# Weights of the last chunk's first block product through the staging buffer, and halves of products read ahead of activation low parts

## What is computed

```python
    merged = jax.nn.sigmoid(ga) * y_a + jax.nn.sigmoid(gb) * y_b
    x = x + merged @ w_o

    h2 = rmsnorm(x, g_ffn)
    x = x + jnp.square(jax.nn.relu(h2 @ w_up)) @ w_down
    return x
```

## Time and profile before

| | us |
|---|---|
| median of 3 runs | 1888.57 (1887.17 to 1890.57) |
| the profiled execution | 1888.48 |
| its span, first to last instruction | 1886.4 |
| TensorE busy | 1865.5 (99% of the span) |
| VectorE busy | 1255.6 (67%) |
| ScalarE busy | 837.2 (44%) |
| GpSimd busy | 129.4 (7%) |

### The profile page before, as it was taken

One profiled execution on the slowest core, in us unless ns is written; L12 is line 12 of the kernel. 1 busy time (PEld: TensorE's weight loads), 2 busy tenths in 40 slices (PEclk: granted clock), 3 DMA queues, 4 the chain that ended last, 5 costly groups with the idle time before them and its releaser, 6 DMA issues.

```text
span 1886.4 us, 22990 instructions
## 1 busy us (share of the span) xinstructions
PE 1865.5 (99%) x9064; PEld 1549.7 (82%) x9064; DVE 1255.6 (67%) x1858; ACT 837.2 (44%) x1234; POOL 129.4 (7%) x104
## 2 busy tenths in 40 slices
PE   9999999999999999999899999999999999999997
PEld 7888888887888888888788888888878888888886
DVE  5356778767456666767863568788665575676777
ACT  7325465464223333434472255554632233344344
POOL 0001111100000000000000112111000000000100
PEclk9999999999999999999999999999999999999999
DMA  4543233333333465564626333233243334655655
GB/s 146 200 159 120 83 89 118 90 93 104 120 101 114 132 134 136 150 136 125 145 88 240 96 104 104 77 118 104 68 146 101 101 112 113 141 148 134 134 147 121
DMA packets 208235, 230.64 MB, mean 122 GB/s; under 512 B 13440, under 2 KB 160640, under 8 KB 207360
## 3 DMA queue, kind: packets, MB, share of 16 engines
q1 hardware_dynamic: 190512, 194.74, 32.7%
q0 software_dynamic: 16896, 33.56, 10.5%
q10 hardware_dynamic: 720, 0.87, 0.1%
HBM read 215.38 MB, written 13.77 MB: 121 GB/s over the span
## 4 chain that ended last, share of the span: by engine, by line
PE 85%; issue 6%; DVE 4%; DMA 3%; ACT 2%; POOL 0%; SPq 0%; POOLq 0%; ACTq 0%; DVEq 0%
PE pj L1816 19%; PE pj L1818 19%; PE pj L1817 19%; DMA gh<-in_w_down 2%; PE yr L2122 1%; PE yr L2124 1%; PE yr L2126 1%; DVE w_lo L1140 1%; PE pt L2122 1%; PE pt L2124 1%; PE pt L2126 1%; PE sc L2122 1%; PE sc L2124 1%; PE sc L2126 1%; PE yr L1923 1%
## 5 line engine op out<-in xcount | busy, mean ns | idle before, releaser
L1816 PE MATMUL pj<-h_hi,w_hi 128*128 128x512 f32 x1408 | 554.4, 394 | 1.0 <-DVE sA L1515 1.0
L1818 PE MATMUL pj<-h_hi,w_lo 128*128 128x512 f32 x1408 | 548.5, 390 | 0.0
L1817 PE MATMUL pj<-h_lo,w_hi 128*128 128x512 f32 x1408 | 548.3, 389 | 0.0
L1140 DVE TENSOR_TENSOR w_lo<-w_raw,w_hi 128x1024 fp32r<-128x1024 f32 x279 | 329.9, 1220 | 115.1 <-ACT w_hi L687 113.6
L687 ACT CAST w_hi<-w_raw 128x1024 fp32r<-128x1024 f32 x276 | 278.6, 1049 | 270.5 <-PE pj L1818 56.9
L1816 PEld LDWEIGHTS pj<-h_hi,w_hi 128*128 128x128 f32 x1408 | 264.4, 188 | 59.0 <-issue 1.9
L1818 PEld LDWEIGHTS pj<-h_hi,w_lo 128*128 128x128 f32 x1408 | 264.3, 188 | 56.0
L1817 PEld LDWEIGHTS pj<-h_lo,w_hi 128*128 128x128 f32 x1408 | 264.5, 188 | 53.9 <-issue 0.5
L697 ACT CAST w_hi<-gh 128x1024 fp32r<-128x1024 f32 x96 | 96.0, 1050 | 118.2 <-DMA gh<-in_w_down 50.5
L1107 POOL TENSOR_TENSOR rcos<-rot,tables 128x512 f32<-128x512 f32 x64 | 87.6, 1370 | 692.4 <-ACT rot L808 633.8
L1140 DVE TENSOR_TENSOR w_lo<-gh,w_hi 128x1024 fp32r<-128x1024 f32 x96 | 113.1, 1219 | 14.2 <-ACT w_hi L697 14.0
(11 more groups left out here) (339 smaller groups left out, 3102.4 us busy)
## 6 DMA issues: line engine op xcount, KB each, us to landing
w_raw<-in_w_in SPq DMA_DIRECT2D x151, 512.0 KB, 4.7
w_raw<-in_w_up SPq DMA_DIRECT2D x64, 512.0 KB, 4.9
gh<-in_w_down POOLq DMA_DIRECT2D x32, 1024.0 KB, 8.7
gh<-in_w_down SPq DMA_DIRECT2D x16, 1024.0 KB, 5.1
w_raw<-in_w_b SPq DMA_DIRECT2D x16, 512.0 KB, 3.9
w_raw<-in_w_o SPq DMA_DIRECT2D x16, 512.0 KB, 3.9
w_raw<-in_w_down SPq DMA_DIRECT2D x16, 512.0 KB, 4.5
x_scratch<-x SPq DMA_DIRECT2D x2, 2048.0 KB, 10.1
```

The lines of the kernel that those rows point to most:

```text
L1140: nc.vector.tensor_tensor(w_lo[s][:, c], src[:, c], w_hi[s][:, c], ALU.subtract).then_inc(lo_done, 1)
L1816: nc.tensor.matmul(out, w_hi[s][:, wc], acts[0], start=first, stop=False)
L1817: nc.tensor.matmul(out, w_hi[s][:, wc], acts[1], start=False, stop=False)
L1818: return nc.tensor.matmul(out, w_lo[s][:, wc], acts[0], start=False, stop=last)
```

## The change

Two edits, both in the last chunk of each layer alone.

1. D1 is made a "plain" unit, as D2 is: SP loads its quarter of `w_down` into `w_raw` in two DMAs of 512 KB, ScalarE and VectorE take it from there, and the buffer `gh1` with the same quarter (which is still loaded) is only the base for the additions. The addition for D5 no longer waits for VectorE's low parts of D1.
2. `evict_half(i, 0)`, the reading of the current product's first half, is moved ahead of `a_low`.

```diff
+    def plain(c, i):
+        return i == 2 or (c, i) == (CH - 1, 1)
+
     def by_raw(j):
-        return j < M0 or M_SEQ[j - M0][0] == "U" or M_SEQ[j - M0][2] == 2
+        return j < M0 or M_SEQ[j - M0][0] == "U" or plain(*M_SEQ[j - M0][1:])
...
-                def quarter(c):
+                def quarter(c, h):
                     d = raw[:].rearrange("p (k c) -> p k c", k=4)
-                    return [(d[:, m:m + 2, :], w_down_q[l, c, 1, 0][:, m:m + 2, :]) for m in (0, 2)]
+                    return [(d[:, m:m + 2, :], w_down_q[l, c, h, 0][:, m:m + 2, :]) for m in (0, 2)]
...
-                    load(m_unit(l, "D", c, 2), quarter(c))
+                    if plain(c, 1):
+                        load(m_unit(l, "D", c, 1), quarter(c, 0))
+                    load(m_unit(l, "D", c, 2), quarter(c, 1))
...
-                        if kind == "D" and i != 2:
+                        if kind == "D" and not plain(c, i):
                             hi_sum(l, c, i, n)
...
-                    pool.wait_ge(lo_done, m_unit(l, "D", c, behind) * 2 + 2 + UNIT_CREDIT)
+                    if not plain(c, behind):
+                        pool.wait_ge(lo_done, m_unit(l, "D", c, behind) * 2 + 2 + UNIT_CREDIT)
...
                     if last_chunk:
+                        if i != 4:
+                            evict_half(i, 0)
                         for t in {1: (5,), 2: (3,), 5: (6,), 3: (7,), 6: (4,)}.get(i, ()):
                             a_low(c, t)
-                        if i != 4:
-                            evict_half(i, 0)
```

## The result

The changed kernel takes 1899.49 us (median of 4 runs, 1898.39 to 1900.06), the kernel before beside it 1888.07 (1887.17 to 1890.57, 4 runs). The ratio is 1.0058, 95% interval 1.0040 to 1.0075: slower by 11.4 us, with 10 forecast. The profiled execution took 1899.60 with a span of 1897.5, so its span too is 11.1 longer than before.

A forecast was written before the change was run, and what follows sets the result against it. TensorE is busy 1865.5 of 1886.4 us, and the chain from D5's low parts through D6's and D4's additions sets each layer's end. +5.2 (layer 1) and +4.8 (layer 0) on 1888.48 gave 1898.5 us, range 1893.0 to 1901.5.

The forecast's parts named there:

- The chain that sets the end: From D5's low parts through D6's and D4's additions, without slack: time lost at D5 arrives whole, +4.8 and +5.2 us.
- D1's place in the queue: D1's halves stand behind D3's base load in SP's queue: 6.3 us issue to cast, 2.8 us new TensorE idle time.
- the other end: Rival: D1's load not in effect behind the base, taking 3.76 us; +2.7 and +2.3 us, total 1893.5; chance 0.10.
- D2's load: D2's halves wait for D1's low parts, then take 3.76 and 4.14 us to cast; layer 1 low parts end 1845.35.
- VectorE's row of work: VectorE's work after D2's low parts: 3.65 us, then D5's low parts 2.36, ending at 1851.3 in layer 1.
- The early addition: D5's addition waits only for its base, goes some 26 us sooner, and takes the DMA off D5's path.
- cannot be cashed: The early addition's intended gain is lost because VectorE reaches D5's low parts only at 1849.0 in layer 1.
- the 2 us allowed: Layer 0: the early addition may cost D(2, 2)'s loads up to 2 us, with no effect on TensorE.
- The second edit: Half reads first: 1.1 us off each wait at D3 and D7, waited for later at D6 and D4; costed at nothing.
- The clock: TensorE's clock can fall behind D1's 2.8 us wait; D5's low parts do not move: nothing up to 0.5 us per layer.

The follow-up runs named there:

- e1: The kernel before with only the half reads moved ahead of the activation low parts: 1887.39 us against 1887.41, ratio 1.0000.
- e5: The changed kernel with VectorE making D5's low parts ahead of its read of D1's second half and the sum for D3: 1896.36 us, ratio 1.0048.
- e11: The changed kernel with D1's halves loaded early and D5's low parts made sooner, but the second edit undone: 1888.27 us, ratio 1.0005 to the kernel before.
- e3: The changed kernel with SP issuing D1's two half loads ahead of the base load for D3 instead of behind it: 1893.69 us, ratio 1.0032.
- e7: The changed kernel with the addition for D5 waiting again for VectorE's low parts of D1: 1905.14 us, ratio 1.0093.
- e2: The changed kernel with the second edit undone, so only D1's weights go through the staging buffer: 1899.20 us, ratio 1.0062.
- e4: The changed kernel with D1's half loads issued right behind those of D(2, 2), ahead of the base for D3: 1888.80 us, ratio 1.0008.

## Why the prediction was right, and where it was off

*The chain that sets the end* was read rightly. From the end of D5's low parts to that of D4's it is 24.5 to 25.9 us in both layers of every kernel of the table, while D5's own place moves over 10 us (16.3 to 26.4); and from the end of D4's low parts in layer 1 to the end of the span it is 14.7 to 14.8 us in all thirteen traces. The forecast's +4.8 and +5.2 at D5 came out as +5.2 and +5.7. e1 shows that time won at D3 and D7 alone does not reach the end, e5 that time won at D5 does. That this chain has no slack holds for these kernels; in e11 it may no longer do so.

*D1's place in the queue.* Forecast: 6.3 us from issue to cast, 2.8 us of idle time. Measured: 6.1, and 2.52 and 2.66. e3 gives the price of the other end (4.1 us, 1893.7). The Trainium skill ("DMA: Bandwidth & Descriptors", Queues, rings and completion order) says that on each DMA engine descriptors are consumed in ring order; e3 agrees, with 4.1 us ahead of the base and 6.1 behind it.

*D2's load* is the mis-sized term. I took 3.76 and 4.14 us to the cast, from D(2, 2) in layer 0 of the kernel before. I left out its twin in layer 1, with 3.7 and 4.6, and the page's median for these loads, from issue to landing:

```profile
w_raw<-in_w_down SPq DMA_DIRECT2D x16, 512.0 KB, 4.5
```

Measured from the freed half to the cast, it was 4.0 and 4.9 in layer 0, 5.2 and 5.1 in layer 1, with nothing else issued at the time. From the end of D1's low parts to that of D2's it is 7.2 and 7.4 us, where the working had 6.5. D1's were 0.3 sooner than worked out, so D2's low parts end at 17.4 and 17.5 instead of 16.9, 1.1 us over the two layers; VectorE's shorter row gave 0.3 of it back, and the sum fell 0.9 short at D5. Why this half load is slower than the other was not settled; the DMA engines' rate during it was a little lower (in layer 1 315 and 311 GB/s in its two fullest microseconds, against 328 and 379 at D(2, 2)).

*VectorE's row of work* between D2 and D5: 5.9 us by the working (1845.35 to 1851.25), 5.7 measured.

*The early addition.* "Takes the DMA away from D5's path" was right, and so was that D5's high parts then wait for VectorE. That its gain "cannot be cashed" was wrong, as e7 shows: 3.2 and 1.4 us at D5. The sum was not hurt, since it priced the loads with an empty queue, but it did so without naming what kept it empty. The other side of it, beside D(2, 2)'s loads, was larger than the 2 us allowed and was still covered. SP and ScalarE in layer 1:

```profile
1816.42 1.50 SPq L478 DMA_DIRECT2D w_raw<-in_w_down  x2
```

```profile
1823.31 1.05 ACT L692 CAST w_hi<-w_raw 128x1024 fp32r<-128x1024 f32 x1 [7.61 <-DMA w_raw<-in_w_down]
```

That is 6.9 us where it was 3.7 before. In both layers of the three traces in which the addition for D5 is not early (before, e1, e7) it is 3.7 to 3.9, and in the ten in which it is, 6.0 to 8.1. TensorE does not wait for it.

*The second edit*, costed at nothing: 0.0 by itself (e1), and on top of the first the changed kernel is 0.3 us slower than e2, within the scatter.

*The clock.* It did fall behind D1's wait, as the stretches table of the changed kernel shows (columns as in the earlier trace rows):

```profile
1843.10:1846.40 3.30, 3.30 (x9) 2.62 (x10) 3.30 (x4) 0.74 (x1) 0.00 (x0) 0.55 0.65 179
```

0.55 is almost wholly the 1.2 GHz level, in D1, right behind 2.66 us without a matmul; in layer 0 D1 had it too, and D4 in layer 1, three stretches where the kernel before had one. It cost TensorE busy time (1871.2 against 1865.5) and not the end. From D2's low parts to D5's it is 5.7 us in both layers of the changed kernel, with D1 at the lower level, and 5.7 in e3 and e4, whose traced executions never fell to it; and the 14.7 to 14.8 us behind D4's low parts in layer 1 are the same with D4 at that level, as in the changed kernel, and without.

## What to carry to other kernels

Ask of a transfer that is moved to another buffer not only what it costs but what stands ahead of it in the queue of the engine that issues it, and by whose work that queue is held: here one position in SP's order was worth 5 to 6 us, and 9 to 10 us of earliness 10 to 11. Follow the shift to the one step that the end hangs on, and put the change's effect at that step, not at the waits that look largest; a wait ahead of TensorE that goes away comes back at the next product when a chain of DMAs paces them all. When an early transfer seems to earn nothing, look at what it would fall on if it were late.

## What was not expected of the hardware

A DMA that adds into its destination and plain loads on another queue get in each other's way: the 1024 KB addition took 10.8 and 12.5 us from issue to use beside two 512 KB loads (e7) and 8.8 alone, and the first 512 KB load of D(2, 2) took 6.0 to 8.1 us beside an addition and 3.7 to 3.9 without, over thirteen traces. And a 512 KB load with no other transfer queued ahead of it took 3.7 to 4.6 us from issue to use in one place (D(2, 2) of the kernel before) and 4.0 to 5.2 in another (D2 of the changed kernel).
